# Two layers of a hybrid RWKV-7, Mamba-2 and attention encoder: projections between the RWKV products as whole-array or 64x64 matmuls

## What is computed

```
x += 1/2 * g0 * RMSNorm_post(SwiGLU_a(mod0(RMSNorm_pre(x))))
x +=       g1 * RMSNorm_post(HybridMixer(mod1(RMSNorm_pre(x))))
x += 1/2 * g2 * RMSNorm_post(SwiGLU_b(mod2(RMSNorm_pre(x))))
```

```
g = jax.nn.sigmoid(p_g).reshape(bsz, s, N_BRANCH, D_MODEL)
merged = g[:, :, 0] * (y_r @ w_br_r) + g[:, :, 1] * (y_m @ w_br_m) + g[:, :, 2] * (y_d @ w_br_d)
return merged @ w_out, v_first
```

## Time and profile before

| | |
|---|---|
| three runs, us | 2736.98, 2737.28, 2739.47 |
| profiled execution, us | 2737.22, its span 2735.5 |
| TensorE (PE) busy | 2620.0 us, 96% of the span |
| VectorE (DVE) busy | 1413.6 us, 52% |
| ScalarE (ACT), GpSimd (POOL) busy | 499.4 us, 232.0 us |
| granted TensorE clock, mean | 0.993 of full speed |
| instruction queue | 236 packets, 3.87 MB |

### The profile page before, as it was taken

The page is one execution under the profiler, slowest core; times in us unless marked ns, Lnnn a source line. Parts: engine busy times, 40 slices in busy tenths (PEclk is TensorE's granted clock), DMA queues, the critical chain, the costliest instruction groups (busy, mean ns, idle before and its releaser), DMA issues.

```text
span 2735.5 us, 66483 instructions
## 1 busy us (share of the span) xinstructions
PE 2620.0 (96%) x30077; PEld 1906.3 (70%) x30077; DVE 1413.6 (52%) x2560; ACT 499.4 (18%) x1016; POOL 232.0 (8%) x372
## 2 busy tenths in 40 slices
PE   6999999999999999999999999999999899999999
PEld 6777877777775555577787778777778745546776
DVE  3552465677775856312035425456787768562001
ACT  1000223122222332100010011322222223221000
POOL 6000102000001101100000010110000011100000
PEclk9999999999999999999999999999999999999999
DMA  9894433322327542484469734423222275424452
GB/s 364 309 337 151 133 117 123 111 83 92 116 80 239 169 168 94 144 291 165 157 242 340 271 128 142 152 91 113 87 83 88 91 253 191 143 96 154 138 168 93
DMA packets 226348, 445.12 MB, mean 163 GB/s; under 512 B 7545, under 2 KB 102327, under 8 KB 226065
## 3 DMA queue, kind: packets, MB, share of 16 engines
q1 hardware_dynamic: 211376, 395.59, 41.5%
q0 software_dynamic: 12960, 38.98, 4.5%
q10 hardware_dynamic: 1728, 6.29, 0.6%
HBM read 422.88 MB, written 17.96 MB: 161 GB/s over the span
## 4 chain that ended last, share of the span: by engine, by line
PE 81%; DVE 11%; ACT 3%; issue 2%; DMA 2%; POOL 1%; DVEq 0%; ACTq 0%; SPq 0%; POOLq 0%
PE ps L1039 79%; DVE scratch L2228 5%; DVE scratch L2231 2%; DVE scratch L2234 1%; DVE gbc L2234 1%; PE ps L1068 1%; DVE scratch L2544 1%; DMA scratch<-in_ada_w 1%; DMA ring<-in_w_in 1%; DMA scratch<-acs_scratch 0%; DMA acs_scratch<-scratch 0%; ACT scratch L2053 0%; ACT scratch L2051 0%; ACT scratch L2200 0%; DVE x L2234 0%
## 5 line engine op out<-in xcount | busy, mean ns | idle before, releaser
L1039 PE MATMUL ps<-hT,ring 64*64 64x256 f32 (+3 forms) x9472 | 1147.9, 367 | 8.3 <-issue 3.1
L1039 PEld LDWEIGHTS ps<-hT,ring 64*64 64x64 f32 (+2 forms) x9472 | 943.0, 160 | 155.9 <-issue 35.8
L1039 PE MATMUL ps<-scratch 64*64 64x32 f32 (+6 forms) x15264 | 846.7, 255 | 56.8 <-DVE scratch L2228 16.1
L1039 PEld LDWEIGHTS ps<-scratch 64*64 64x64 f32 (+2 forms) x15264 | 592.6, 140 | 332.3 <-issue 206.2
L2228 DVE TENSOR_TENSOR scratch<-scratch,ps 128x256 f32<-128x256 f32 (+3 forms) x314 | 155.2, 494 | 661.1 <-ACT scratch L1895 533.1
L1039 PE MATMUL ps<-ring,hT 64*64 64x256 f32 (+2 forms) x2816 | 425.4, 421 | 5.3 <-DVE scratch L2234 2.6
L1039 PEld LDWEIGHTS ps<-ring,hT 64*64 64x64 f32 (+1 forms) x2816 | 228.7, 149 | 143.3 <-issue 116.8
L2228 DVE TENSOR_TENSOR scratch<-scratch 128x512 f32<-128x512 f32 (+4 forms) x426 | 276.1, 648 | 75.4 <-ACTq L2035 31.8
L1039 PE MATMUL ps<-ring,scratch 128*128 128x512 f32 x512 | 234.7, 593 | 0.5
L2234 DVE SCALAR_TENSOR_TENSOR scratch<-scratch,ccol 128x1024 f32<-128x1024 f32 x120 | 154.2, 1285 | 15.2 <-DMA scratch<-in_ada_w 11.3
L1895 ACT ACTIVATE scratch<-ps 128x512 f32<-128x512 f32 x40 | 23.9, 597 | 746.1 <-PE ps L1039 746.1
(11 more groups left out here) (228 smaller groups left out, 1392.8 us busy)
## 6 DMA issues: line engine op xcount, KB each, us to landing
ring<-in_w_in SPq DMA_DIRECT2D x56, 2048.0 KB, 9.0
ring<-in_ffn_w SPq DMA_DIRECT2D x88, 1024.0 KB, 9.0
scratch<-in_ada_w SPq DMA_DIRECT2D x35, 2048.0 KB, 16.2
scratch<-in_ffn_w SPq DMA_DIRECT2D x44, 1024.0 KB, 5.0
...
```

The costliest lines, as they stand in the source:

```text
L1039: return pe.matmul(o, lhsT, rhs, start=start, stop=stop)
```

## The change

- Of the 14 items that were made on tiles, only the steps at the points of the state chain (`TILE_POINTS`) stay on tiles, in multiples of four per item; all others are made on the whole array (`fill_mixed` in place of `fill_tiles`). An item may be made in both forms.
- `FILL` has another order, `FILL_PAIR` another number of steps at each point: among others six instead of four at `s2` in six pairs, 10 and 3 in pairs 4 and 5 instead of 1 to 3 for the long segments and levels, and eight at the last pair's `end`.
- The first convolution moves from pair 2 to pair 1, with three taps in each of its levels. ScalarE makes the convolution's sigmoid ahead of the first taps of the item that it has just emptied.
- GpSimd computes the norm's power before it issues the next pair's loads.
- Attention: one product more before the transposes of `on`, two more before the last head's maps are turned; the merges of Mamba's halves are cut by token tile and placed inside heads 2, 3, 5 and 6; the end is regrouped by token tile, and `w_out`'s first half is loaded in two parts.
- ScalarE instead of VectorE copies the first layer's parameters, and ScalarE instead of SyncE issues the loads of `w2`.

Cut to its core (`silu_order` in place of counted numbers, the merges' new helpers and the renamed output functions are left out):

```diff
-FILL = [("z", 0), ("z", 1), ("z", 2), ("z", 3), ("c", 0), ("q", 0), ("c", 1), ("q", 1), ("c", 2), ("q", 2),
-        ("c", 3), ("q", 3), ("c", 4), ("c", 5), ("v", 0), ("v", 1)]
+FILL = [("z", 0), ("z", 1), ("z", 2), ("c", 0), ("z", 3), ("c", 1), ("q", 0), ("c", 2), ("q", 1), ("c", 3),
+        ("q", 2), ("c", 4), ("q", 3), ("c", 5), ("v", 0), ("v", 1)]
...
-FILL_PAIR = ((8, 8, 8, 2, 2, 2, 2, 0, 2, 0, 1, 1, 4, 1, 2, 0, 2, 2, 3),
-             (14, 10, 10, 3, 3, 3, 3, 0, 2, 0, 1, 1, 4, 1, 2, 0, 2, 2, 3),
-             (14, 10, 10, 3, 3, 3, 3, 0, 2, 0, 1, 1, 4, 1, 2, 0, 2, 2, 3),
-             (14, 10, 10, 3, 3, 3, 3, 0, 2, 0, 1, 1, 4, 1, 2, 0, 2, 2, 3),
-             (14, 8, 7, 1, 2, 2, 2, 0, 1, 0, 1, 1, 3, 1, 1, 0, 1, 1, 3),
-             (11, 8, 8, 2, 2, 2, 2, 0, 2, 0, 1, 2, 4, 2, 2, 0, 2, 2, 9),
-             (8, 8, 8, 2, 2, 2, 2, 0, 2, 0, 1, 1, 4, 1, 2, 0, 2, 2, 3),
-             (14, 8, 7, 1, 2, 2, 2, 0, 1, 0, 1, 1, 3, 1, 1, 0, 1, 1, 0))
+FILL_PAIR = ((7, 8, 8, 2, 2, 2, 3, 0, 2, 0, 1, 1, 6, 1, 2, 0, 2, 2, 2),
+             (13, 7, 6, 2, 2, 2, 2, 0, 1, 0, 1, 1, 4, 1, 1, 0, 1, 1, 2),
+             (13, 8, 7, 2, 2, 2, 2, 0, 2, 0, 1, 2, 6, 1, 2, 0, 2, 2, 3),
+             (13, 8, 8, 2, 2, 2, 2, 0, 2, 0, 1, 1, 6, 1, 2, 0, 2, 2, 2),
+             (13, 10, 10, 3, 3, 3, 3, 0, 2, 0, 1, 1, 6, 1, 2, 0, 2, 2, 2),
+             (13, 10, 10, 3, 3, 3, 3, 0, 1, 0, 1, 1, 4, 1, 1, 0, 1, 1, 2),
+             (12, 7, 7, 2, 2, 2, 2, 0, 2, 0, 1, 1, 6, 1, 2, 0, 2, 2, 2),
+             (13, 8, 7, 2, 2, 2, 2, 0, 2, 0, 1, 2, 6, 1, 2, 0, 2, 2, 8))
+TILE_POINTS = ("r0", "u0", "s1", "r1", "u1", "s2", "r2", "u2", "s3", "r3", "u3")
...
+def tile_steps(i):
+
+    on_tiles = [False] * sum(c for _, c in FILL_EARLY)
+    for row in FILL_PAIR:
+        for point, c in zip(FILL_POINTS, row):
+            on_tiles += [point in TILE_POINTS] * c
+    steps = on_tiles[2 * UNIT_STEPS * i:2 * UNIT_STEPS * (i + 1)]
+    kept = sum(steps) // 4 * 4
+    return [on and sum(steps[:n]) < kept for n, on in enumerate(steps)]
...
-CONV_AT_LEVELS = CONV_SIGMOID = {2: 0, 3: 1, 4: 2, 5: 3, 6: 4, 7: 5}
+    return sum(2 if n in FFN_ITEMS or n == IT_OUT else 1 for n in range(item) if n % 2 == parity)
+
+
+CONV_AT_LEVELS = CONV_SIGMOID = {1: 0, 3: 1, 4: 2, 5: 3, 6: 4, 7: 5}
...
+                w_o = row(a["w_out"], l)
+                out_slot = ring[:, IT_OUT % 2, 0:KT * 512].rearrange("p (k n) -> p k n", k=KT)
+                sp.wait_ge(*bm_part(l, 5))
+                sp.dma_start(out_slot[:, 0:6, :], kmaj(w_o[:, 0:6 * P, 0:512])).then_inc(slot_loaded[IT_OUT % 2].sem, 16)
+                sp.wait_ge(*group_done(l, group_of(IT_OUT - 2) + 1))
+                sp.dma_start(out_slot[:, 6:8, :], kmaj(w_o[:, 6 * P:8 * P, 0:512])).then_inc(slot_loaded[IT_OUT % 2].sem, 16)
+                load(l, IT_OUT + 1, (IT_OUT + 1) % 2, kmaj(w_o[:, :, 512:1024]), free_after=group_of(IT_OUT - 1) + 1)
...
+                    group_norm_rstd(q - 2)
                     next_pair(q)
-                    group_norm_rstd(q - 2)
-                    if q == 2:
+                    if q == 3:
...
+                def fill_mixed(i):
+
+                    on_tiles = tile_steps(i)
+                    split = sum(on_tiles) // 4
+                    tiles = [(turn, h, k) for turn in range(2) for k in range(split) for h in range(2)]
+                    whole = [(r, h, k) for k in range(split, KT) for r in range(2) for h in range(2)]
+                    order = [tiles.pop(0) if on else whole.pop(0) for on in on_tiles]
+                    begun = set()
                     pe.wait_ge(*fill_evac(l, 2 * i))
+                    for n, (on, (x, h, k)) in enumerate(zip(on_tiles, order)):
+                        if on and (x, h, k) == (1, 0, 0):
                             pe.wait_ge(*fill_done(l, 2 * i + 1))
+                        for r in range(2) if on else (x,):
+                            first, last = r not in begun, not any(o or y == r for o, (y, _, _) in zip(on_tiles[n + 1:], order[n + 1:]))
+                            begun.add(r)
+                            part = (r + x) % 2
+                            rows = slice(64 * part, 64 * part + 64) if on else slice(0, P)
+                            for cols in (slice(0, 64), slice(64, P)) if on else (slice(0, P),):
+                                w, m = fill_operands(i, r, h, k, rows, cols)
+                                ins = mm(ps[cols, FILL_BANKS[r], h * S:(h + 1) * S], w, m, first, last)
+                        if n == 2 * UNIT_STEPS - 1 or (on and (x, h, k) == (0, 1, split - 1)) or (split == 0 and n == 0):
+                            ins.then_inc(fill_done.sem, 1)
+                        yield
...
+                    late = KT - 1
+                    first = [(0, k, t) for k in range(late) for t in range(TT)] + [(1, k, 0) for k in range(late)]
+                    behind = [(0, late, 0), (0, late, 1), (1, late, 0)] + [(1, k, 1) for k in range(KT)]
+                    for h, k, t in first + behind:
                         item = IT_BD + h
                         g, par = group_of(item), item % 2
-                        pe.wait_ge(*slot_loaded[par](l, loads_before(item, par) + 1))
-                        bank_free(l, g)
-                        steps = [(k, t) for k in range(KT) for t in range(TT)]
-                        for k, t in sorted(steps, key=lambda kt: kt[::-1]) if h else steps:
-                            if h == 0 and t == 0:
-                                pe.wait_ge(*yd_ready(l, k + 1))
-                            if h and (k, t) == (KT // 2, 1):
-                                pe.wait_ge(*hT_ready(l, 3))
-                                turn_tile(0, merged).then_inc(merged_turned.sem, 1)
-                            ins = mm(ps[:, 2 * (g % 2) + t, :], ydT[:, k, t * P:(t + 1) * P], slot(par)[:, k, :],
-                                     k == 0, k == KT - 1)
-                            if h and (k, t) == (KT - 1, 0):
-                                ins.then_inc(rows_done.sem, 1)
-                            if t == TT - 1 and k == KT - 1:
-                                ins.then_inc(group_done.sem, 1)
-                            yield
+                        if (k, t) == (0, 0):
...
-                    beside(3 if h == 0 else 2)
+                    beside(4 if last else 3 if h == 0 else 2)
...
-                    beside(4 if h == 0 else 3)
+                    beside(3 if last else 4)
...
+                def down_weights(j):
+
+                    w2 = row(a["ffn_w2"], l)[:, f, j * 256:(j + 1) * 256, :].rearrange("a (k p) n -> p (a k) n", p=P)
+                    act.dma_start(w2s[:, j % 2, :, :], w2).then_inc(w2_loaded[j % 2].sem, 16)
+
+                down_weights(0)
+                down_weights(1)
...
+            act.wait_ge(*params_turned(0, 1))
+            act.activation(prm[:, :], ps[:, 3, :], ACT.Identity).then_inc(params_evac.sem, 1)
...
+                    if between is not None:
+                        conv_sigmoid(between)
...
-                        fill_evacuations(q - 1, "k3")
-                        if q - 1 in CONV_SIGMOID:
-                            conv_sigmoid(CONV_SIGMOID[q - 1])
+                        fill_evacuations(q - 1, "lv")
+                        fill_evacuations(q - 1, "k3", CONV_SIGMOID.get(q - 1))
...
-                    read_params(0, 3)
                     first_sum(1)
+                    dve.wait_ge(*params_evac(0, 1))
...
-                        if p in CONV_AT_LEVELS:
+                        if p in CONV_AT_LEVELS and p > 1:
                             convolve(2)
...
-                            convolve(2 if d else 4)
+                            convolve((4 if d else 0) if p == 1 else (2 if d else 4))
...
-                            convolve(2)
+                            convolve(3 if p == 1 else 2)
...
+                    if h == 6:
+                        mamba_added(1, 0)
...
+                    if h in (2, 3):
+                        mamba_gated(0, h - 2)
+                    if h == 6:
+                        mamba_gated(1, 1)
...
+                    if h in (2, 3):
+                        mamba_added(0, h - 2)
+                    if h == 5:
+                        mamba_gated(1, 0)
+                    if h == 6:
+                        mamba_added(1, 1)
...
+                gated_rows(IT_BD, 1, 2, sg_first, 0, 0)
+                own.step(added_rows(sg_first, 0, 0))
+                gated_rows(IT_BD, 1, 2, sg_first, 1, 0)
+                raised(added_rows(sg_first, 1, 0), hT_ready(l, 3))
+                gated_rows(IT_BD, 1, 2, sg_first, 0, 1)
+                evacuated(l, added_rows(sg_first, 0, 1), out_group - 2)
+                merged_to_channels(0)
+                gated_rows(IT_BD, 1, 2, sg_first, 1, 1)
+                evacuated(l, added_rows(sg_first, 1, 1), out_group - 1)
+                merged_to_channels(1)
```

125 lines of the change are left out of this document (58 added, 67 removed).

## The result

| | before | changed |
|---|---|---|
| median, us (10 runs each) | 2737.37 (2734.29 to 2742.14) | 2751.85 (2738.72 to 2760.72) |
| ratio | | 1.0047, 95% interval 1.0028 to 1.0066 |
| profiled execution, us | 2737.22 | 2738.72 |
| granted clock of the profiled execution | 0.993 | 0.997 |
| granted clock, mean of the runs | 0.993 (80 runs beside the experiments) | 0.989 |

What follows compares the result with a forecast made beforehand. TensorE, busy 2620 of 2735.5 us, was taken as the bound. Terms 33.4 + 2.2 - 9.2 - 6.0 - 16.0 - 9.6 - 0.7 = -5.9 gave 2731.3 us from a median of 2737.3; range 2710 to 2752.

Steps and rivals of the forecast that it cites:

- drain decides: Rival: 122 whole/tile round trips cost 0.34 us each (41.5), issue gaps hardly shrink; +15, 2752 us, chance 0.2.
- signs of being wrong: Levels no longer than before, over 35 us idle in a pair stretch, or issue gaps under 3 or over 15 us.
- in the levels VectorE is not late: Levels: TensorE never waits for VectorE there, so 64 form round trips at 0.30 us are fully exposed, +19.2 us.
- Term 7: Start and rest: parameter copy moved to ScalarE saves 0.7 us; moved w2 loads and GpSimd's norm power cost 0.
- Term 5, the halved clock: Pair 5, both layers: half clock behind the longest issue gap goes as pair 5's load moves behind its levels, -8.5 us.
- Term 5, the rest: Pairs: waits for the copy of `us` and issue gaps fall from 27.2 to 19.7 us, -7.5.
- Term 1: Fillings: 122 more round trips between whole-array and 64x64 products, 0.20 to 0.34 us each, cost +33.4 us.
- nothing is saved by overlap: Before the levels and in the middle: existing waits for VectorE hide none of 32 round trips, +9.0 us.
- Term 2: Pair 3's first segment: an item ends inside it and TensorE waits for ScalarE to empty both banks, +2.2 us.
- Term 3: Last pair's end, both layers: eight steps fill the 3.18 us wait and end the half clock behind it, -9.2 us.
- Term 4: Two more steps at `s2` in six of eight pairs cover half the wait for the state update, -6.0 us.
- Term 6: Attention heads: extra products and halved merges remove all of TensorE's 4.0 + 4.0 + 1.6 us waits, -9.6 us.

Runs made afterwards that it cites:

- e5: Changed kernel with the first convolution back in pair 2 and GpSimd's last z product one pair earlier, as before: 2727.2 us.
- e15: Changed kernel with GpSimd's last z product held back to pair 2's state chain and two taps instead of three in pair 1's levels: 2736.0 us.
- e1: The changed kernel run again without any edit: 2749.4 us.
- e8: Changed kernel with the earlier tables, whole fillings only at ops and end, seven steps at the last pair's end, five loads per layer held back from the levels: 2716.4 us.
- e9: Changed kernel with only five 2 MB loads of filling items per layer held back from the levels to the state chain's second chunk: 2723.1 us.
- e16: Kernel before the change with only six loads of filling items per layer held back to the state chain's second chunk: 2718.4 us.
- e2: Changed kernel with every filling of the 14 items turned back to 64x64 tiles, the rest as changed: 2738.1 us.

## Why the prediction was wrong

Forecast 2731.3 us, faster by 0.2%; measured 2751.85, slower by 0.5%, just inside the upper end of 2752. The number of the rival "drain decides" (2752) was met, but not its mechanism: its 41.5 us for the form were 9 to 20. That the time lies inside the range is luck, since the range's upper end came from those 41.5 us. Two of the signs of being wrong were met, issue gaps over 15 us (17.1) and pair stretches together more than 10 us longer (10.8); the second was to mean that the drain decided, and e5 shows that the pairs are longer for another reason as well. By the steps:

- **The step that failed is one that isn't there.** The part on the change prices no VectorE work in pair 1: the convolution's move, with three taps where a level has two steps, has no term, and "in the levels VectorE is not late" rests on pair 0, which has no taps before or after. Term 7 moved GpSimd's norm power and its loads but not the `z` product behind them, which went from pair 1 to the start of pair 2. The runs showed waits of 0.69, 1.20 and three of 0.35 us in pair 1's levels and of 2.6 us in front of pair 2, and e5 puts the two with their clock at 22 us. Of these, e15 finds 13 in the number of taps and in the `z` product; why the other 9 hang on the convolution's place stays open.
- **Term 5, the halved clock (-8.5), had the wrong sign.** The gap of 2.41 us in pair 5 shrank to 0.90 and the half clock behind it went, but new waits of 1.2 to 2.6 us in both layers brought more: 0.989 instead of 0.993, some 5 to 7 us. I took the clock's cost from one execution; its length is different in each. Half of each stretch, 1.7 us per 3.4, was also too much: the pairs of e1 lost 0.37 us per microsecond of half clock, 1.3 per 3.4.
- **Term 5, the rest (-7.5):** the copy wait fell by 7.7, issue by 1.8; right within 2 us. That blocks of instructions come late beside a 2 MB load was right, e8, e9 and e16 show it. That fewer instructions relieve it is right too (9 us from e2 to the changed kernel), but the new tables added 7.
- **Term 1 (+33.4)** was right in the array (0.31 us per level, about 30 us busy) and wrong in the sum: "nothing is saved by overlap" failed. Net it is 11.3 in this kernel. (By its own 0.30 us the 32 round trips are 9.6, not 9.0.)
- **Term 2 (+2.2):** waits for the evacuation rose by 2.9, from 2.2 to 3.8 + 1.3, with 1.27 us at pair 3 for the 1.4 forecast and two of 0.63 beside it in each layer. **Term 3:** the wait of 3.18 us is gone, its half clock in the first profile too; in e1 10.2 us of half clock stood in pair 7 of layer 1. **Term 4 (-6.0):** -7.0. **Term 7's start (-0.7):** -0.9 at the first feed-forward's end.
- **Term 6 (-9.6)** was right. Head 0's first transposes to the first of `merged` took 97.27 us in both layers and take 1119.51 - 1027.11 = 92.40, twice 4.87:

```profile
1027.11 0.60 PE L1766 MATMUL ps<-ident,scratch 128*128 128x128 f32 x4
...
1119.51 1.04 PE L1070 MATMUL ps<-ident,merged 128*128 128x128 f32 x8
```

With the measured sizes: -9.7 (attention) - 0.9 - 5.8 (term 3 without clock) - 5.2 (the copy of `us` in e2, 3.1 us instead of 8.3) - 6.3 (state update in e2) + 2.9 (evacuation in e2) + 7.2 (issue in e2) + 22 = 4.2, where e2 stood 3.0 us above before; and 11.3 for the form makes 15.5, where 14.5 were measured. This was added up after the fact, from single profiles, and is a check of the book-keeping and no test.
